# Two transformer blocks on one core: a norm with residual and the norm behind it in one stage, the memory's and the context's rows turned and normalised beside products

## What is computed, as far as it matters

```python
def rms_norm(x, gain):
    y = x * lax.rsqrt(jnp.mean(x * x, axis=-1, keepdims=True) + 1e-6)
    return y * gain
# first block, behind the mixers
x = x + rms_norm(merged @ w_out, norm_mix_post)
h = rms_norm(x, norm_xa_pre)
mem_n = rms_norm(mem, norm_mem)
xa = memory_cross_attention(h, mem_n, wq, wk, wv, wo)   # k = mem_n @ wk, v = mem_n @ wv, q = h @ wq
x = x + rms_norm(xa, norm_xa_post)
h = rms_norm(x, norm_ffn_pre)
f = conv_ffn(h, w_up, conv_w, conv_b, w_down)            # ends in a product with w_down
x = x + rms_norm(f, norm_ffn_post)
# second block, before its first mixer: tokens and context, both normalised and modulated
h     = rms_norm(x,   g) * (1 + scale) + shift
h_ctx = rms_norm(ctx, g) * (1 + scale_ctx) + shift_ctx
```

## Time and profile before

| | us |
|---|---|
| median of 3 runs (2573.59 to 2577.34) | 2576.7 |
| the profiled execution's own time | 2581.72 |
| its span, first to last instruction | 2579.3 |
| PE busy in it | 2301.4 |
| VectorE, ScalarE, GpSimd busy | 631.7, 477.9, 196.1 |

### The profile page before, as it was taken

One profiled execution on the slowest core, in us unless ns is written; L12 is line 12 of the kernel. 1 busy time (PEld: TensorE's weight loads), 2 busy tenths in 40 slices (PEclk: granted clock), 3 DMA queues, 4 the chain that ended last, 5 costly groups with the idle time before them and its releaser, 6 DMA issues. The chain is left out here.

```text
span 2579.3 us, 26865 instructions
## 1 busy us (share of the span) xinstructions
PE 2301.4 (89%) x11316; PEld 1524.4 (59%) x11316; DVE 631.7 (24%) x1455; ACT 477.9 (19%) x889; POOL 196.1 (8%) x256
## 2 busy tenths in 40 slices
PE   6999696876999699888998899999979689999997
PEld 5755385565888575567877544454448554544453
DVE  2556112012220223562221211111110221111112
ACT  1222401111220233533331100000011120000000
POOL 2023001001111112310001000000000100000000
PEclk9999697998999789997887999999989889999998
DMA  5469542222443111010006699999954369999993
GB/s 192 163 247 332 211 172 82 98 75 89 139 155 105 65 66 65 34 46 20 1 2 246 289 427 428 427 426 427 427 193 163 134 267 427 426 428 427 427 427 148
DMA packets 120019, 575.55 MB, mean 223 GB/s; under 512 B 5152, under 2 KB 28281, under 8 KB 95321
## 3 DMA queue, kind: packets, MB, share of 16 engines
q1 hardware_dynamic: 118431, 570.59, 55.6%
q0 software_dynamic: 768, 2.02, 0.4%
q10 hardware_dynamic: 698, 1.18, 0.2%
HBM read 572.72 MB, written 1.05 MB: 222 GB/s over the span
## 5 line engine op out<-in xcount | busy, mean ns | idle before, releaser
L426 PE MATMUL linear_ps<-hT,ring 128*128 128x256 f32 x1344 | 300.3, 387 | 39.0 <-PEq L345 18.3
L426 PEld LDWEIGHTS linear_ps<-hT,ring 128*128 128x128 f32 x1344 | 260.6, 194 | 78.4 <-issue 41.7
L2485 PE MATMUL ex_u<-ring_extra,ex_xt 128*64 128x512 f32 x1024 | 224.3, 592 | 3.0 <-DMA ring_extra<-in_w 3.0
L2485 PE MATMUL ex_u<-ring,ex_xt 128*64 128x512 f32 x1024 | 223.9, 592 | 1.5 <-issue 1.5
L1651 PE MATMUL dl_front<-dn_src,ring 128*128 128x256 f32 (+1 forms) x512 | 177.4, 503 | 2.0 <-DVE dp_cv L1818 2.0
L2485 PEld LDWEIGHTS ex_u<-ring_extra,ex_xt 128*64 128x64 f32 x1024 | 74.9, 137 | 148.7 <-issue 148.7
L2485 PEld LDWEIGHTS ex_u<-ring,ex_xt 128*64 128x64 f32 x1024 | 75.2, 137 | 145.1 <-issue 145.1
L1113 PE MATMUL ffn_ps<-hT,ring 128*128 128x256 f32 x704 | 155.2, 384 | 5.9 <-PEq L345 5.9
L1113 PEld LDWEIGHTS ffn_ps<-hT,ring 128*128 128x128 f32 x704 | 135.8, 193 | 25.3 <-issue 6.3
L2574 DVE TENSOR_TENSOR ex_hid<-ex_sil,ex_u 128x512 f32<-128x512 f32 x32 | 34.6, 1082 | 425.3 <-PE ex_u L2485 425.3
L1651 PEld LDWEIGHTS dl_front<-dn_src,ring 128*128 128x128 f32 x512 | 99.3, 199 | 65.8 <-issue 58.9
(11 more groups left out here) (493 smaller groups left out, 2775.1 us busy)
## 6 DMA issues: line engine op xcount, KB each, us to landing
ring<-in_w SPq DMA_DIRECT2D x96, 2048.0 KB, 19.0
ring_extra<-in_w SPq DMA_DIRECT2D x96, 2048.0 KB, 20.7
ring<-in_ada_w SPq DMA_DIRECT2D x24, 2048.0 KB, 8.4
ring<-in_ffn_w_up SPq DMA_DIRECT2D x22, 1024.0 KB, 6.5
ring<-in_w_in SPq DMA_DIRECT2D x8, 2048.0 KB, 8.8
ring<-in_w_in_a SPq DMA_DIRECT2D x8, 2048.0 KB, 8.2
ring<-in_w_in_b SPq DMA_DIRECT2D x6, 2048.0 KB, 20.7
ring<-in_ffn_w_down SPq DMA_DIRECT2D x5, 2048.0 KB, 8.8
```

The source lines that it names most:

```text
L426: mm = pe.matmul(ps[:, q % banks, 0:n], w[:, k, j * P:(j + 1) * P], src[:, k, 0:n], start=k == 0, stop=k == kc - 1)
L2485: mm = pe.matmul(u[H * a:H * a + H, i, :], xt[:, b, k, H * a:H * a + H], w[a][:, 512 * k:512 * k + 512], start=k == 0, stop=k == KC - 1, s ...
```

## The change

- A new `stage_renorm` does a norm with residual and the norm behind it in one stage. DVE scales in place, POOL adds chunks 0 to 4 to `xT` and DVE 5 to 7, ACT squares `xT` in pairs as they come, PE adds them in a second bank. It stands three times: after w_out, after wo and after the down product, the last with the shift of the second block.
- After w_out it takes the keys' products as `fill`: chunks 0 to 2 between the two sums on PE, 3 to 7 behind the second.
- `turn_rows` and the norm of its rows become the class `Rows`, whose steps go beside products. The memory's transfer is issued by ACT in the merge stage; on PE its turning stands ahead of w_out's chunk 0 and its sum ahead of chunk 4, ACT's squares ahead of moving chunk 2 and its root ahead of chunk 6, DVE's part behind `ada_finish`. The context's transfer is issued by ACT at the head of `stage_ffn_up`; in `stage_ffn_down` PE turns it ahead of f = 2 and sums ahead of f = 8.
- The down product uses four banks, two chunks to each, and is moved out in four.
- The buffers of memory, keys, queries and values are made earlier; three buffers of `stage_delta` lie in `dn_src`, which lives longer.

```diff
-def turn_rows(K, dram, dst, name, rows=None):
...
+class Rows:
...
+    def load(self, eng, dram):
+        landed = self.K.counter("rows_landed", 16)
+        eng.dma_start(self.rows, dram.rearrange("(a p) d -> p a d", p=P)).then_inc(landed.sem, landed.tick())
+    def begin(self, st):
...
+        self.ps = K.ps("rows_ps", [P, 2, 512], st)
+    def turn(self, pe):
+        pe.wait_ge(self.landed.sem, self.landed.count)
...
+    def sum(self, pe):
+        for c in range(KC):
+            if c % 4 == 0:
+                pe.wait_ge(self.squared.sem, self.squared.at(c // 4 + 1))
+            mm = pe.matmul(self.ps[:, 0, 0:T], self.K.ones[:, :], self.dst[:, c, :], start=c == 0, stop=c == KC - 1)
+        mm.then_inc(self.summed.sem, self.summed.tick())
+    def square(self, act):
+        act.wait_ge(self.moved.sem, self.moved.at(4))
+        for i in range(2):
+            act.activation(self.dst[:, 4 * i:4 * i + 4, :], self.raw[:, 4 * i:4 * i + 4, :], ACT.Square,
+                           scale=D ** -0.5).then_inc(self.squared.sem, self.squared.tick())
+    def root(self, act):
+        act.wait_ge(self.summed.sem, self.summed.at(1))
+        act.activation(self.K.rstd[:, :], self.ps[:, 0, 0:T], ACT.Sqrt, bias=self.K.epsb[:, :]).then_inc(self.rooted.sem, self.rooted.tick())
+    def shift_rows(self, act):
+        for c in range(KC):
+            act.wait_ge(self.normed.sem, self.normed.at(c + 1))
+            act.activation(self.dst[:, c, :], self.dst[:, c, :], ACT.Identity, bias=self.shift(c))
+    def on_dve(self, dve):
...
+        dve.wait_ge(self.moved.sem, self.moved.at(4))
+        dve.wait_ge(self.rooted.sem, self.rooted.at(1))
+        dve.reciprocal(K.rstd[:, :], K.rstd[:, :]).then_inc(own.sem, own.tick())
+        dve.wait_ge(own.sem, own.count)
+        for c in range(KC):
+            dve.scalar_tensor_tensor(out=self.dst[:, c, :], in0=self.raw[:, c, :], scalar=self.gain(c), in1=K.rstd[:, :],
+                                     op0=ALU.mult, op1=ALU.mult).then_inc(self.normed.sem, self.normed.tick())
...
+def stage_renorm(K, y, post, dst, pre, shift=None, fill=None):
...
+    g0 = K.used
+    tiles = 2 if fill else 0
+    by_pool = 5
+    with K.stage() as st:
+        ss = K.ps("norm_ss", [P, 2, 512], st)
+        ps = K.ps("linear_ps", [P, 4, 512], st) if fill else None
+        block = st.enter_context(nc.Block())
+        pair = lambda t, i: t[:, 2 * i:2 * i + 2, :]
+        @block.scalar
+        def _(act):
+            def move(q):
+                act.wait_ge(full.sem, full.at(q + 1))
+                fill[1](act, q // 4, q % 4, ps[:, q % 4, 0:T]).then_inc(free.sem, free.tick())
+            for i in range(2):
+                act.activation(dst[:, 4 * i:4 * i + 4, :], y[:, 4 * i:4 * i + 4, :], ACT.Square,
+                               scale=D ** -0.5).then_inc(squared.sem, squared.tick())
+            act.wait_ge(summed.sem, summed.at(1))
+            act.activation(K.rstd[:, :], ss[:, 0, 0:T], ACT.Sqrt, bias=K.epsb[:, :]).then_inc(rooted.sem, rooted.tick())
+            for i in range(4):
+                if fill and i in (1, 3):
+                    move(i // 2)
+                act.wait_ge(added.sem, added.at(min(2 * i + 2, by_pool)))
+                if 2 * i + 2 > by_pool:
+                    act.wait_ge(added_last.sem, added_last.at(2 * i + 2 - by_pool))
+                act.activation(pair(dst, i), pair(K.xT, i), ACT.Square, scale=D ** -0.5).then_inc(squared.sem, squared.tick())
+            if fill:
+                move(2)
+            act.wait_ge(summed.sem, summed.at(2))
+            act.activation(K.rstd[:, :], ss[:, 1, 0:T], ACT.Sqrt, bias=K.epsb[:, :]).then_inc(rooted.sem, rooted.tick())
+            for q in range(3, KC if fill else 0):
+                move(q)
+            for c in range(KC if shift else 0):
+                act.wait_ge(normed.sem, normed.at(c + 1))
+                act.activation(dst[:, c, :], dst[:, c, :], ACT.Identity, bias=shift(c))
+        @block.tensor
+        def _(pe):
+            def chunk(q):
+                w = K.tile(pe, g0 + q // 4, KC)
+                if q >= 4:
+                    pe.wait_ge(free.sem, free.at(q - 3))
+                for k in range(KC):
+                    mm = pe.matmul(ps[:, q % 4, 0:T], w[:, k, (q % 4) * P:(q % 4 + 1) * P], fill[0][:, k, :], start=k == 0, stop=k == KC - 1)
...
+            for c in range(KC):
+                if c % 4 == 0:
+                    pe.wait_ge(squared.sem, squared.at(c // 4 + 1))
+                mm = pe.matmul(ss[:, 0, 0:T], K.ones[:, :], dst[:, c, :], start=c == 0, stop=c == KC - 1)
+            mm.then_inc(summed.sem, summed.tick())
+            for q in range(3 if fill else 0):
+                chunk(q)
+            for c in range(KC):
+                if c % 2 == 0:
+                    pe.wait_ge(squared.sem, squared.at(2 + c // 2 + 1))
+                mm = pe.matmul(ss[:, 1, 0:T], K.ones[:, :], dst[:, c, :], start=c == 0, stop=c == KC - 1)
+            mm.then_inc(summed.sem, summed.tick())
+            for q in range(3, KC if fill else 0):
+                chunk(q)
+        @block.vector
+        def _(dve):
+            dve.wait_ge(rooted.sem, rooted.at(1))
+            dve.reciprocal(K.rstd[:, :], K.rstd[:, :]).then_inc(own.sem, own.tick())
+            dve.wait_ge(own.sem, own.count)
+            for c in range(KC):
+                dve.scalar_tensor_tensor(out=y[:, c, :], in0=y[:, c, :], scalar=post(c), in1=K.rstd[:, :],
+                                         op0=ALU.mult, op1=ALU.mult).then_inc(scaled.sem, scaled.tick())
+            dve.wait_ge(scaled.sem, scaled.at(KC))
+            for c in range(by_pool, KC):
+                dve.tensor_tensor(K.xT[:, c, :], y[:, c, :], K.xT[:, c, :], ALU.add).then_inc(added_last.sem, added_last.tick())
+            dve.wait_ge(rooted.sem, rooted.at(2))
+            dve.reciprocal(K.rstd[:, :], K.rstd[:, :]).then_inc(own.sem, own.tick())
+            dve.wait_ge(own.sem, own.count)
+            for c in range(KC):
+                dve.scalar_tensor_tensor(out=dst[:, c, :], in0=K.xT[:, c, :], scalar=pre(c), in1=K.rstd[:, :],
+                                         op0=ALU.mult, op1=ALU.mult).then_inc(normed.sem, normed.tick())
+        @block.gpsimd
+        def _(pool):
+            for c in range(by_pool):
+                pool.wait_ge(scaled.sem, scaled.at(c + 1))
+                pool.tensor_tensor(K.xT[:, c, :], y[:, c, :], K.xT[:, c, :], ALU.add).then_inc(added.sem, added.tick())
+        @block.sync
+        def _(sp):
+            K.issue(sp, g0 + tiles)
+    K.used = g0 + tiles
...
+                    if (t, j) in act_steps:
+                        act_steps[t, j](act)
...
-def stage_merge(K, o_attn, o_ssm, gates, dst):
+def stage_merge(K, o_attn, o_ssm, gates, dst, mem):
...
+        @block.scalar
+        def _(act):
+            mem.load(act, K.io["mem"][0])
...
-def stage_ffn_up(K, src, hid):
+def stage_ffn_up(K, src, hid, context):
...
+            context.load(act, K.io["ctx_2"][0])
...
-def stage_ffn_down(K, hid, dst, extra):
+def stage_ffn_down(K, hid, dst, extra, context):
...
-        ps = K.ps("down_ps", [P, KC, 512], st)
+        ps = K.ps("down_ps", [P, KC // 2, 2, T], st)
+        context.begin(st)
...
+                if f == 2:
+                    context.turn(pe)
+                if f == 8:
+                    context.sum(pe)
                 for c in range(KC):
-                    mm = pe.matmul(ps[:, c, 0:T], w[:, f % per, c * P:(c + 1) * P], hid[:, f, :],
-                                   start=f == 0, stop=f == FC - 1)
+                    mm = pe.matmul(ps[:, c // 2, c % 2, :], w[:, f % per, c * P:(c + 1) * P], hid[:, f, :],
+                                   start=f == 0 and c % 2 == 0, stop=f == FC - 1 and c % 2 == 1, skip_group_check=True)
                 mm.then_inc(full.sem, full.tick())
                 K.done_at[g0 + f // per] = full.count
         @block.scalar
         def _(act):
+            context.square(act)
+            context.root(act)
+            context.shift_rows(act)
             act.wait_ge(full.sem, full.at(FC))
-            for c in range(KC):
-                act.activation(dst[:, c, :], ps[:, c, 0:T], ACT.Copy).then_inc(taken.sem, taken.tick())
+            for c in range(0, KC, 2):
+                act.activation(dst[:, c:c + 2, :], ps[:, c // 2, :, :], ACT.Copy).then_inc(taken.sem, taken.tick())
+        @block.vector
+        def _(dve):
+            context.on_dve(dve)
...
+                K.ada["ps"], K.ada["t_ps"] = K.ps("ada_ps", [P, 512], banks), K.ps("ada_t", [P, 512], banks)
...
+            memT, turned_mem, kT, qT = (K.sb(n, [P, KC, T], ctx=K.part) for n in ("memT", "mem_turned", "xa_kT", "xa_qT"))
+            values = K.sb("xa_v", [P, TT, D], ctx=K.part)
+            mem = Rows(K, values[:, :, :], turned_mem, memT, gain("norm_mem"))
+            stage_merge(K, o_attn, o_ssm, proj[:, 16:32, :], K.hT, mem)
```

(65 more changed lines are left out.)

137 lines of the change are left out of this document (55 added, 82 removed).

## The result

The changed kernel takes 2502.1 us (median of 4 runs, 2491.86 to 2503.9) against 2575.1 for the kernel before in the same comparison: ratio 0.971, interval 0.968 to 0.974. The gain was forecast as 60 us off a median of 2576.7; it is 74.6 from there and 73.0 between the two medians of this comparison. Two executions of the whole study, one of the kernel before at 3139.6 us and one of b_pause6 at 5989.6, lie far outside all the others and are left out everywhere.

A forecast was written before the change was run, and what follows sets the result against it. PE, busy 89% of the span, was taken as the bound, with time won where it stands. Gains of 23.3 + 14.3 + 4.9 + 17.4 + 0.2 = 60.1 us off the median 2576.7 gave 2516.6, range 2508 to 2527.

The forecast's parts named there:

- The edited part: From w_out to the second block's first product: the terms for the moved work gain 60.1 us together.
- rival 3: New norm stages: POOL and DVE shut each other out, a pair of adds taking 1.13 us; 3.6 us more, chance 0.03.
- Rival 4: w_out's tail ends late by a table-load delay the rows don't show; 1.3 us later, chance 0.03.
- rival 1: w_out and down product: inserted turnings and sums pay their own stage's price; 5.3 us more, chance 0.12.
- rival 5: Whole change: one late input stalls whole products on PE, half the gain goes; about 2546 us, chance 0.05.
- rival 6: w_out to the queries: PE runs at 1.2 GHz without its pauses; slower, 2622 us, chance 0.03.
- The level in the norms: Behind wo: merged norms take 22.7 us instead of 27.6, a gain of 4.9, second sum priced at the low clock.
- rival 2: The two unfilled new stages: PE stays at 2.4 GHz, so sums are shorter; 4.5 us less, 2512, chance 0.10.
- The step that failed: From the second block's first product on: everything as before but shifted, with no gain or loss.
- the prediction's own last sign: Behind the second block: a stretch changing by over 3 us would prove a step wrong.

The follow-up runs named there:

- b_pause6: Kernel before with a stage of six short ACT instructions ahead of the delta stage; ratio 0.999, median of nine runs 2568.7 us.
- a_again: The changed kernel run once more without an edit, for a second profile; 2492.1, 2492.1, 2495.1 and 2503.7 us.
- b_pause3: Kernel before with a stage of three short ACT instructions ahead of the delta stage; ratio 0.998, median 2567.6 us.
- b_alloc: Kernel before with only the delta stage's three buffers moved into the longer-lived `dn_src`; ratio 0.999.
- b_again: Kernel before run once more without an edit, for a second profile; ratio 1.001.
- b_early3: Kernel before with the stage of three short ACT instructions ahead of the up product instead, 540 us before the delta stage; ratio 1.003, median 2582.1 us.
- b_warm: Kernel before with 24 extra products of constants that nothing reads, ahead of PE's waits in the delta stage; ratio 0.999.
- a_ctxown: Changed kernel with the context turned and normalised in its own stage behind the last new stage; 2530 to 2531 us in three runs, 2519.5 in the fourth.
- a_warm: Changed kernel with 24 extra products of constants that nothing reads in the delta stage; ratio 0.974, 2494.3 us and three runs at 2507.
- a_nofill: Changed kernel with the keys' products in a stage of their own instead of as fill; 2508.3 to 2509.3 us.
- a_pause6: Changed kernel with a stage of six short ACT instructions ahead of the delta stage; 2498.8 us and three runs from 2508.3 to 2510.3.
- a_keep: Changed kernel with products of constants that nothing reads where PE stands in the two unfilled new stages; ratio 0.973, 2495.5 to 2505.2 us.
- a_pause3: Changed kernel with a stage of three short ACT instructions ahead of the delta stage; 2491.3, 2513.3, 2514.7 and 2518.0 us.
- a_ctxpause3: Changed kernel with the context in its own stage and three short ACT instructions ahead of the delta stage; six runs, median 2516.7 us.

## Why the prediction was wrong

**The edited part: right.** Turning beside w_out took 3.0 us instead of 3.8 (361.80 to 364.83), the sums 3.5 as priced, and the down product with its moves grew by 6.7 for 7.1. The eight scalings, five of them beside POOL's adds, took 5.61 for an estimate of 5.6, so rival 3 fell: five pairs at 1.13 would have ended 1.4 us later. Rival 4 fell as well: the load at 389.61 takes 1.28, stands right behind a move and its ACTIVATE starts at 390.91. Nothing of rivals 1, 5 and 6 is seen.

**The level in the norms: half right.** I took the first sum behind wo at 3.72, as in the profile before. In the first profile after it took 5.25 and the second 6.95, where 3.7 and 6.7 were priced; so the stage gained 3.0 and not 4.9. In a_again the same lines read:

```profile
548.84 3.72 PE L489 MATMUL norm_ss<-hT,ones 128*128 128x256 f32 x16 [2.56 <-ACT hT L454]
...
569.67 3.75 PE L1259 MATMUL ffn_ps<-hT,ring 128*128 128x256 f32 x8 [5.91 <-PEq L441]
```

From squares to the up product 21.9, a gain of 5.7. That is rival 2, and it happens in some executions. The executions come in two types by the time at which the merge starts, 326 or 332 us, in both kernels (eight of the sixteen profiles each). Against the before-type profile with the early merge (b_pause3), a_again gains 67.2 up to the front, where the late type gives 60.5. By the times, four of the changed kernel's eight runs (2491.9 to 2495.1) are of the early type. So rival 2 at 0.10 was too low; it is about as likely as the other. Its price was 4.5 us, of which only 3.3 are in its listed terms.

**The step that failed** is the one sentence that carried no sum: "from the second block's first product on, everything as before but shifted". A shift was costed at nothing. The delta stage took 14.5 us less in the profile, and the prediction's own last sign, a stretch behind the second block that changes by over 3 us, came true. The place of the tiles did not do it (b_alloc). What differs is where in the stage PE is granted 1.2 GHz. Worked out from the granted clock in slices of 1 us, the sixteen profiles show these patterns:

| profiles | clock falls, us into the stage | back at 2.4 | next fall | stage, us |
|---|---|---|---|---|
| before, b_again, b_early3, b_warm, a_ctxown | 6.2 to 6.3 | 23.3 to 23.4 | 30.1 to 30.2 | 190 to 194 |
| after, a_again, b_alloc, a_warm, a_nofill | 9.2 to 9.3 | 22.8 to 23.0 | none up to 100 | 179 to 180 |
| the five with a pause just ahead | low from before the start | 3.1 to 4.5 (a_pause6: 23.1) | 7.4 to 11.3 | 176 to 188 |
| a_keep | 5.5 | 19.1 | 29.4 | 185 |

So the two forms part in the stage's first 10 us: a first fall 3 us earlier comes with a second fall that the short form doesn't have. PE does not stand just ahead of the first one. In the kernel before it is busy without a gap, with products of 64x32 and 128x128 in turn, before the fall and across it:

```profile
1162.40:1165.50 3.10, 3.10 (x21) 2.29 (x21) 1.42 (x6) 0.00 (x0) 0.00 (x0) 1.00 0.51 188
1165.50:1169.30 3.80, 3.80 (x25) 3.16 (x26) 0.77 (x4) 1.25 (x5) 0.00 (x0) 0.51 0.00 0
```

Edits ahead of the stage, with none inside it, change the form. Two microseconds of pause took the long form away in the kernel before (b_pause3: 181.2) and from the kernel with the context's stage (193.7 to 181.1), and made the changed kernel's stage longer (a_pause3: 188.1). That the moment of the start does it, and not PE's level or work just ahead, is the reading that b_early3 favours; it was argued and not shown.

In the kernel before, most executions get the long form, by their times. In the changed kernel all eight timed runs lie at 2504 or below, and the one at 2503.9 had 179.1. With the late merge and the long form it would be about 2515 to 2518 (2503.9 and 11 to 14.5 more); with the early merge 2506.9 (a_ctxown's profiled execution, 2519.5, less 12.6). So none had the long form, though forms in between, as the 188.1 of a_pause3, can't be excluded for the runs without a profile. The forecast of 2516.6 is thus about what the changed kernel would take with the long form and the late merge. That it missed the median by 14.5, the very figure of the stage, is chance: between the profiled executions' own times, 2581.72 and 2503.9, the gain is 77.8, and 3.2 of it come from another place.

**The second such term:** 3.2 us came between the two expert layers. Before, the norm's first sum stands after one instruction, for nothing that the profile shows:

```profile
1901.48 0.48 PE L370 MATMUL norm_ss<-hT,ones 128*128 128x256 f32 x1 [4.00 <-ACT hT L356]
...
1905.06 5.75 PE L370 MATMUL norm_ss<-hT,ones 128*128 128x256 f32 x15 [3.09 <-issue]
```

and in the changed kernel's first profile it doesn't:

```profile
1827.64 6.06 PE L408 MATMUL norm_ss<-hT,ones 128*128 128x256 f32 x16 [4.28 <-ACT hT L394]
```

All profiles of the kernel before and its variants have 1133.8 to 1134.2 us for this part; the changed ones have 1130.6 to 1130.9, but for a_warm and a_keep, which add PE instructions and have 1133.8 and 1134.0. In this pair the products behind the norm start 3.1 us earlier against the first expert product, which is the 3.2. But the account isn't whole: in a_pause3, a_pause6, a_nofill, a_ctxown and a_ctxpause3 PE stands too, 0.73 to 1.63 us after 5 to 7 instructions of that sum, and their part is no longer. The stand moves along with small edits to what PE is given before, which fits a fixed place in PE's instruction stream; that was not tested, and its cause is open.

**The range** failed with it. Its lower end was rival 2's 2512.1 less 3.1, which is 2509 and not 2508, and the 3.1 was the spread of three runs. The ten of b_again reach 11.7 us below their median, so the kernel before had already shown no more than a part of its own spread.

**What stays open:** which rule picks the level. The starts and lengths of the sixteen profiles give no simple one (1099.5 us has the short form and 1100.9 the long one, 1154.6 the long one and 1156.7 the short one), the share of a form was only counted in 4 to 10 runs of each variant, and extra products in the stage didn't force the short form. A pause that moves the start and leaves PE's level just ahead alone was tried once (b_early3), in the kernel before only.

## What to carry to other kernels

Count a change's gain up to the last stage whose work it moves, and give the stages behind it a term of their own when they are chains of small products at a granted clock well below 1: the same work took 176 to 194 us here by what lay ahead of it. Take several profiles before reading a difference there, and the spread for a range from more than three runs; a single one of b_alloc would have named the wrong cause. A norm that must stand alone is worth merging and filling: the fill gave 16.7 us and the moved context 12.6, each 0.6 to 0.7 us above the range priced from the rows.

## What the runs showed of the hardware that I had not expected

A stage whose instructions and order are the same runs in forms of 176.4, 179, 181, 183, 185, 188, 190 and 193 us, at a granted clock of 0.92 down to 0.81, and a wait of 2 us ahead of it can shorten the whole kernel by 10 to 14. The forms are exact: five profiles of four kernels have the clock's first fall at 6.2 to 6.3 us into the stage, five others at 9.2 to 9.3. The level fell at 1165.5 us though PE had been busy without a gap for the 6.2 us before. The executions of the kernel before fall into groups (2559.5 to 2566.5, 2573.5 to 2580, 2581 to 2583), with none of 71 from 2567 to 2573. After the same pause of 2.56 us the same sum of 16 instructions took 3.72 in one execution, at a granted clock of 1.00, and 5.25 in another, at 0.71. And PE can stand for 3.1 us in a stage whose instructions nobody edited, in one kernel and not in another with the same 11316 PE instructions.
